# An expert layer whose 64 slots are filled through a permutation instead of in order

## The reference

```python
pg = softmax(t @ w_rg); g_prob, g_idx = top_k(pg, 1)           # one of 4 groups
e_prob, e_idx = top_k(softmax(le_sel), 2)                      # two of its 8 experts
combine = sum(one_hot(g_idx * 8 + e_idx, 32) * e_w[..., None], axis=1)
a = einsum('nd,edf->nef', t, w_g); u = einsum('nd,edf->nef', t, w_u)
y = einsum('nef,efd->nd', silu(a) * u * combine[..., None], w_d)
```

## Time and profile before

| | us |
|---|---|
| median of three runs | 999.95 (999.56 to 1001.64) |
| span of the profiled execution | 995.7 |
| PE busy | 836.0 (84%) |
| DVE, POOL, ACT busy | 342.1, 164.7, 140.4 |
| mean traffic | 326 GB/s, 324.54 MB |
| queue of SP and its share of 16 engines' span | 287.84 MB, 73.5% |
| POOL's queue (gathers, scatters and others) | 21.86 MB, 6.2% |

### The profile page before, as it was taken

How to read it: one execution, slowest core, us unless ns; L and a number is a source line. 1 busy time by engine, 2 the same in 40 slices (tenths; PEclk the granted TensorE clock), 3 DMA queues, 4 the chain that set the end, 5 groups by cost and what they waited for, 6 DMA issues and landing times.

```text
span 995.7 us, 12750 instructions
## 1 busy us (share of the span) xinstructions
PE 836.0 (84%) x4891; PEld 426.4 (43%) x4891; DVE 342.1 (34%) x832; ACT 140.4 (14%) x327; POOL 164.7 (17%) x250
## 2 busy tenths in 40 slices
PE   3899999998997998997878788998599878787854
PEld 2556566665466333332333235647433323232321
DVE  3113555556586111111101138568511110111136
ACT  1122222224010111110101021101111100110110
POOL 1041112123111120111111100130201111111000
PEclk9999999999997899998989999998599998999988
DMA  9997594358259996999999959968899999999941
GB/s 335 366 370 267 181 336 155 111 213 308 86 215 366 394 389 261 418 420 418 419 419 418 410 224 389 339 214 313 340 400 417 417 420 418 419 419 419 383 170 63
DMA packets 91756, 324.54 MB, mean 326 GB/s; under 512 B 12654, under 2 KB 25678, under 8 KB 67608
## 3 DMA queue, kind: packets, MB, share of 16 engines
q1 hardware_dynamic: 73936, 287.84, 73.5%
q0 software_dynamic: 12704, 21.86, 6.2%
q10 hardware_dynamic: 5032, 13.71, 3.5%
HBM read 313.62 MB, written 32.05 MB: 347 GB/s over the span
## 4 chain that ended last, share of the span: by engine, by line
PE 47%; DMA 31%; DVE 14%; issue 4%; ACT 2%; POOL 2%; SPq 1%; POOLq 0%; ACTq 0%; DVEq 0%
DMA ring<-in_w_expert_up 17%; PE psum L1016 15%; PE psum L896 8%; PE psum L1038 5%; DMA h_hT<-in_w_expert_up 5%; PE psum L868 3%; DMA arena<-h_scratch,gidx 3%; PE psum L792 3%; PE psum L843 3%; DMA y_scratch<-arena,sidx 2%; DMA ring<-in_w_ada 2%; PE psum L1000 2%; DMA m_scratch<-m 1%; DVE stats L1488 1%; PE psum L947 1%
## 5 line engine op out<-in xcount | busy, mean ns | idle before, releaser
L1016 PE MATMUL psum<-ring,arena 128*64 128x512 f32 x880 | 263.8, 647 | 36.7 <-DMA ring<-in_w_expert_up 27.7
L1016 PEld LDWEIGHTS psum<-ring,arena 128*64 128x64 f32 x880 | 87.0, 148 | 170.9 <-issue 167.7
L1038 PE MATMUL psum<-ring,arena 128*64 128x512 f32 x440 | 125.8, 603 | 20.2 <-DVE arena L1797 19.5
L1793 DVE TENSOR_TENSOR arena<-arena,psum 128x256 f32<-128x256 f32 x34 | 14.3, 421 | 292.4 <-ACT arena L1351 292.4
L1016 PE MATMUL psum<-h_hT,arena 128*64 128x512 f32 x208 | 96.4, 619 | 10.5 <-DMA ring<-in_w_expert_up 9.6
L896 PE MATMUL psum<-ring,h_hT 128*128 128x384 f32 x288 | 96.5, 488 | 0.0
L843 PE MATMUL psum<-ring,h_hT 128*128 128x512 f32 x160 | 69.3, 593 | 1.8 <-ACT h_hT L1436 1.5
L896 PEld LDWEIGHTS psum<-ring,h_hT 128*128 128x128 f32 x288 | 53.6, 191 | 34.1
L652 POOL DMA_INDIRECT y_scratch<-arena,sidx x32 | 32.6, 1020 | 214.8 <-DVE arena L1803 214.8
L1038 PEld LDWEIGHTS psum<-ring,arena 128*64 128x64 f32 x440 | 36.0, 137 | 71.4 <-issue 46.9
L1803 DVE COPY arena<-psum 128x512 f32<-128x512 f32 x32 | 22.1, 691 | 122.2 <-PE psum L1038 122.2
(11 more groups left out here) (215 smaller groups left out, 883.9 us busy)
## 6 DMA issues: line engine op xcount, KB each, us to landing
ring<-in_w_expert_down SPq DMA_DIRECT2D x52, 1024.0 KB, 25.3
ring<-in_w_expert_gate SPq DMA_DIRECT2D x50, 1024.0 KB, 16.5
ring<-in_w_expert_up SPq DMA_DIRECT2D x50, 1024.0 KB, 23.0
ring<-in_w_ada SPq DMA_DIRECT2D x24, 2048.0 KB, 14.0
h_hT<-in_w_expert_gate SPq DMA_DIRECT2D x12, 1024.0 KB, 18.1
h_hT<-in_w_expert_up SPq DMA_DIRECT2D x12, 1024.0 KB, 23.2
h_hT<-in_w_expert_down SPq DMA_DIRECT2D x12, 1024.0 KB, 26.0
ring<-in_w_qkv SPq DMA_DIRECT2D x9, 1024.0 KB, 12.5
```

The lines of the kernel that those rows point to most:

```text
L1016: last = pe.matmul(bank[b][64 * e:64 * e + 64, :].rearrange("p (g n) -> p g n", g=2), mem.GT[b][:, c, 64 * e:64 * e + 64], w, start=(c == ...
L1038: last = pe.matmul(bank[5 + half][64 * e:64 * e + 64, :], mem.actT[b][:, f, 64 * e:64 * e + 64], w[:, f, 512 * half:512 * half + 512], sta ...
```

## The change

`rank_of_slot()` is new and gives, for each of the 64 slots, the place in the expert's list that stands there. `row64` becomes that vector. Everything else in the program is the same: same instructions, same shapes, same transfers.

```diff
+def rank_of_slot():
+    rank = np.zeros(CAP)
+    for r in range(CAP):
+        group, turn = r % 8, r // 8
+        place = 4 * ((group >> 2) ^ (turn >> 1 & 1)) + ((group >> 1 & 1) + 2 * (turn & 1) + (turn >> 2)) % 4
+        rank[8 * group + place] = r
+    assert sorted(rank) == list(range(CAP))
+    return rank
...
-    put("row64", np.tile(np.arange(CAP), (P, 1)))
+    put("row64", np.tile(rank_of_slot(), (P, 1)))
```

## The result

The changed kernel takes 990.0 us (987.72 to 991.87) against 999.75 (995.64 to 1001.64) of the kernel before, beside which it ran: a ratio of 0.9907, with a 95% interval of 0.9883 to 0.9931. A second set of the same kernel on another chip gave 990.37 us and 0.9896 (0.9865 to 0.9927). The span of the profiled execution fell from 995.7 to 988.2 us. The new function adds 12 lines above the program, so line 1016 of before is 1028 of after, 1038 is 1050, and 415 is 427.

The account below looks back on a forecast made before the run. Late in each layer, weight transfers at full DMA share decide, landing with their slowest engine. Lag 10.1 plus exposed transfers 1.5 gives 11.6 us off 999.95: 988.35, say 988.4 us, range 983.0 to 996.0.

Parts of the forecast that it names:

- What bounds the kernel: Late in each layer expert weights decide at DMA share 1.02; uneven engines delay the last down by 8.1 and 7.4 us.
- First term, the lag: At each layer's end, the slowest engine's distance behind the average falls to 2.7 us, gaining 5.4 + 4.7 = 10.1 us.
- gather-free tail: Slowest engine's distance behind the average for a load at 134.5 us, ending a busy stretch without gathers: 1.3 us.
- The count by the router's lists: Rows on the fullest engine by the skill's rule: 81 and 83 before, 55 and 61 after, for layers 0 and 1.
- Second term, the exposed transfers: Six gathers and scatters on the chain each end 0.25 us sooner, 1.5 us together.
- Third, what is late next: At the layers' ends PE follows the earlier landings; deciding `up` lands 5 to 6 and 10 us earlier.
- Full removal: Rival: distance at the layers' ends falls to 1.3 us and six transfers save 0.5 each; 15.9 us gained, 984.1; chance 0.18.
- PE as the next bound: Rival: only the wait before each layer's deciding pair disappears, 2.3 us on average; 5.6 us gained, 994.4; chance 0.15.
- only bytes count: Within the no-change rival (chance 0.11): gathers and scatters cost by bytes whatever the slots, so time stays at 1000.
- a row packet gets dearer: Rival: far-apart partitions make each row packet cost more in saturated stretches; at 0.1 us more, 7.6 us slower, 1007.6; chance 0.05.

Follow-up runs that it names:

- no_rows: Kernel before with row numbers set beyond the bound, so all 66 gathers and scatters are issued but move no rows; 968.4 us.
- the two halves: Changed kernel with the changed constant in one layer only, slots in order in the other: layer 1 alone 994.4 us, layer 0 alone 994.7 us.
- quads: Changed kernel with another permutation: place r goes to four-slot group g = r mod 8 (slots 4g to 4g+3, then 32+4g to 32+4g+3); 988.2 us.
- snake: As quads, but every second turn of eight places runs backwards; 988.8 us.
- spread_again: The changed kernel run once more, unaltered, beside the others on the same chip; 990.4 us.
- heap: Changed kernel with another permutation: places 0 to 7 in slots 0 to 3 and 32 to 35, the next eight in 4 to 7 and 36 to 39; 1017.1 us.
- stride8: Changed kernel with another permutation: place r goes to slot 8 x (r mod 8) + r div 8; 1006.0 us.

## Why the prediction was right, point by point

The forecast was 988.4 us, a gain of 11.6; measured are 9.75 by the medians and 9.3 by the ratio, and 990.0 lies in the range of 983.0 to 996.0.

**What bounds the kernel.** Right. The readings that a full DMA share hides uneven engines, and that the staircase at a layer's end measures it, held in every run that works the rows in full: within the noise, the time rises with the sum of the two lags. One reading was wrong. The chain of before holds eight indirect transfers and not six: the earlier trace rows leaves out a scatter at 399.23 (9.04 us) and a gather at 409.88 (8.16 us).

**First term, the lag, 5.4 + 4.7 = 10.1 us.** The mechanism is shown by the permutations and by `no_rows`, and that it comes once in each layer by the two halves. The size of the gain was a little high. I took 2.7 us as left; 3.9 and 3.6 were left, so the lag fell by 4.2 + 3.8 = 8.0 us. The mis-sized part is that remainder: 1.3 of the gather-free tail and 1.4 for lists that do not divide. The working let an engine have at most one row more than another in a transfer; I did not count that the 64 slots of even and odd experts load different engines, and that their lists differ in length. The count by the router's lists in the text beside it, 2.5 and 4.1 us of surplus, already included that; with the 1.3 it makes 3.8 and 5.4, right in layer 0 and too much in layer 1. (The count of layer 0 leaves out the 15 rows beyond place 63. With them the fullest engine has 89 rows before and 58 after, against a mean of 48.)

**Second term, the exposed transfers, 1.5 us.** Not borne out by this pair of profiles, and not settled. The first gather of layer 0 went from 8.36 to 7.26 us and the last scatter of layer 0 from 2.84 to 2.22; the first gather of layer 1 stayed (5.43 and 5.45), its last scatter went from 4.37 to 4.59. The gather of the further pass took longer, 10.31 us instead of 9.44, and the two that the prediction missed took 8.97 and 8.31 us instead of 9.04 and 8.16. The scatter at 356.07 is no longer on the chain. The seven that stand on both chains take 47.6 us before and 47.1 after, 0.5 us less. The first gather of layer 0 took 7.26 in one profile of the changed kernel and 9.16 in the other, so a single one tells little.

**Third, what is late next.** Right for layer 0, only just for layer 1. The deciding `up` of layer 0 landed at 561.9, 3.9 us earlier, where the prediction had 5 to 6, and that of layer 1 at 927.4, 8.0 us earlier, where it had 10. In layer 1 PE was then no longer waiting for it. From the landing at 911.5 to the last scatter the chain above has PE, with short steps of DVE between, and no wait for a transfer: its gate and up took 10.00 us, partly at the lower clock (8.80 before), and it reached the last gate and up at 927.50, level with the landing. The last wait is gone from the chain in `quads` and `snake` as well; in `spread_again` it is still there, and layer 1 took 240.8 us instead of 241.4 to 241.6. So in layer 1 the earlier landing has met PE, and landing earlier still would there have gained little.

Layer 0 became 8.3 us shorter and layer 1 3.2 in the profile. In layer 0 this is more than the lag's 4.2, and the surplus lies ahead of the bound stretch. From the first gather's issue to the down at 394 us there are 394.03 - 313.47 = 80.6 us before and 394.40 - 317.64 = 76.8 after. 1.1 us of it is the gather. Another part is work at the lower clock that this execution of before happened to have: its gate and up of the first pair took 10.00 us against 8.78, and a down took 5.34 against 3.67. Single matmuls of that down took 1.11 and 1.06 us; at the full clock the same matmul takes 0.59 us. I would not count that as the change's. Over the four kernels dealt in both layers, layer 0 took 264.7 us on average (263.2 to 266.2) and layer 1 241.3 (240.8 to 241.6). With slots in order it was 271.6 and 270.7 for layer 0 and 244.6 and 244.7 for layer 1. That makes 6.5 and 3.3 us, together 9.8, about what was measured (9.3 and 10.4 by the two ratios). The lags give 8.0 of it. That the total came nearer to the forecast than this is in part luck: some 2 us of layer 0 lie ahead of its end, and no run places them.

**The rivals.** Full removal was excluded by the remaining 3.9 and 3.6 us. PE as the next bound did not come at its price (994.4): PE still waits for `up`, 26.2 us in the page's costliest group, where it was 27.7. Its sign, a wait gone from the chain, did come at the end of layer 1, where it costs at most the 0.6 us between a lag 3.8 us shorter and a layer 3.2 us shorter. That only bytes count is refuted by `heap` and `stride8`. That a row packet gets dearer is refuted by POOL's queue in the same stretch of 135 us, against the earlier trace rows: the same 2.69 MB at the same 5.7% of the engines.

```profile
q0 software_dynamic: 2595, 2.69, 5.7%
```

The transfers themselves land sooner, 9.0 and 7.8 us at the median against 9.4 and 8.1: 0.3 to 0.4 us each, near the 0.25 that I took, but under cover.

## What to carry to other kernels

A DMA share of 1 says that no engine rests, not that the engines are even. Take the stretch at the end of a bound stage, from the issue of the last large transfer to its landing, and compare the average engine's end with the landing: the difference is the most that an even load would give, once a stage, as long as what waits for that landing is itself ready. Where an indirect transfer leaves slots empty, decide which slots those are by the groups that share an engine, since it costs nothing to deal the rows to all groups in turn, and dealing by the wrong groups, or filling one group after another, cost 7 and 18 us here.

## What the runs showed of the hardware that I had not expected

The unevenness that the queues can absorb has an end: up to a lag of about 8 us all engines stayed busy through the layer (419 GB/s); at 9.5 and 11.8 us the traffic in the middle fell to 414 and 410 GB/s, and the layer's time grew faster than the lag. With the gathers' rows alone the lag was 3.4 to 4.0 us, with those of the scatters added 7.4 to 8.1, against 1.9 to 2.5 with none. So scatters of the same rows from the same slots seem to weigh more than gathers; no run has scatters alone, and none shows why.
